# DeltaNet's V convolved token-major, with accumulating DMAs for the three lagged taps

## The reference

```python
def _causal_depthwise_conv(x, w):          # w is (4, channels)
    return lax.conv_general_dilated(
        x, w[:, None, :].astype(x.dtype), window_strides=(1,), padding=[(CONV_WIDTH - 1, 0)],
        dimension_numbers=('NWC', 'WIO', 'NWC'), feature_group_count=x.shape[-1])

proj = h @ w_in
qkv, z, b_pre, a_pre = _split(proj, L1_SPLITS)
qkv = jax.nn.silu(_causal_depthwise_conv(qkv, conv_w))
q, k, v = _split(qkv, [GDN_QK_W, GDN_QK_W, GDN_V_W])     # 2048, 2048 and 4096 channels
...
rhs = jnp.concatenate([v * beta[..., None], k_beta * jnp.exp(g_cum)[..., None]], axis=-1)
```

## Time and profile before

| | |
|---|---|
| three executions | 2725.23, 2725.53, 2725.72 us |
| span of the profiled execution | 2723.3 us |
| the profiled execution's own time | not given apart from the span; the median of the runs is 2.2 us above it |
| TensorE busy | 2707.9 us, 99% of the span |
| VectorE, ScalarE busy | 1807.0 us (66%), 1412.0 us (52%) |
| GpSimd busy | 94.2 us (3%) |
| DMA | 510.93 MB, mean 188 GB/s |
| granted clock of TensorE | full in all 40 slices |
| the four DeltaNet rounds | about 1226 to 1760 us of the span |

### The profile page before, as it was taken

The page is one execution under the profiler, slowest core; times in us unless marked ns, Lnnn a source line. Parts: engine busy times, 40 slices in busy tenths (PEclk is TensorE's granted clock), DMA queues, the critical chain, the costliest instruction groups (busy, mean ns, idle before and its releaser), DMA issues.

```text
span 2723.3 us, 37074 instructions
## 1 busy us (share of the span) xinstructions
PE 2707.9 (99%) x13198; PEld 2252.4 (83%) x13198; DVE 1807.0 (66%) x2538; ACT 1412.0 (52%) x2005; POOL 94.2 (3%) x80
## 2 busy tenths in 40 slices
PE   9999999999999999999999999999999999999998
PEld 7888888888888888888888888888888888888887
DVE  5554678666666666668797978656767666666444
ACT  5444555444444444458787778554454444444443
POOL 0000000000000000001111111000000000000000
PEclk9999999999999999999999999999999999999999
DMA  8564466766666666666464656555666666666664
GB/s 260 155 195 146 154 198 188 200 193 193 192 193 192 193 190 196 194 188 195 151 191 155 186 178 188 170 182 189 193 193 194 192 193 193 193 193 194 209 194 158
DMA packets 264737, 510.93 MB, mean 188 GB/s; under 512 B 20497, under 2 KB 21265, under 8 KB 264353
## 3 DMA queue, kind: packets, MB, share of 16 engines
q1 hardware_dynamic: 260064, 493.91, 60.0%
q0 software_dynamic: 3152, 11.57, 1.3%
q10 hardware_dynamic: 1392, 3.77, 0.4%
HBM read 503.91 MB, written 5.28 MB: 187 GB/s over the span
## 4 chain that ended last, share of the span: by engine, by line
PE 96%; DVE 2%; ACT 0%; issue 0%; DVEq 0%; DMA 0%; SPq 0%; ACTq 0%
PE acc L602 30%; PE acc L603 30%; PE acc L608 30%; PE aux L843 1%; DVE wlo L1541 1%; PE aux L687 1%; PE aux L855 1%; PE aux L848 1%; PE aux L837 0%; PE aux L829 0%; DVE const L1986 0%; DVE arena L1986 0%; DVE arena L2027 0%; DVE arena L2024 0%; DMA x<-in_x 0%
## 5 line engine op out<-in xcount | busy, mean ns | idle before, releaser
L1541 DVE TENSOR_TENSOR wlo<-wraw,whi 128x1024 fp32r<-128x1024 f32 x928 | 1137.0, 1233 | 711.0 <-ACT whi L1052 704.8
L1052 ACT ACTIVATE whi<-wraw 128x1024 fp32r<-128x1024 f32 x928 | 978.5, 1059 | 1101.8 <-PE acc L608 1059.5
L602 PE MATMUL acc<-whi,hT_hi 128*128 128x512 f32 x2624 | 1033.9, 394 | 0.5 <-ACT arena L1062 0.5
L603 PE MATMUL acc<-whi,hT_lo 128*128 128x512 f32 x2624 | 1022.8, 390 | 0.0
L608 PE MATMUL acc<-wlo,hT_hi 128*128 128x512 f32 x2624 | 702.8, 390 | 0.5 <-DVE wlo L1541 0.5
L608 PEld LDWEIGHTS acc<-wlo,hT_hi 128*128 128x128 f32 x2624 | 492.0, 188 | 103.7 <-DVE wlo L1541 1.3
L602 PEld LDWEIGHTS acc<-whi,hT_hi 128*128 128x128 f32 x2624 | 493.3, 188 | 101.9 <-ACT arena L1062 0.8
L603 PEld LDWEIGHTS acc<-whi,hT_lo 128*128 128x128 f32 x2624 | 493.4, 188 | 100.1
L602 PE MATMUL acc<-whi,arena 128*128 128x512 f32 x1072 | 417.2, 389 | 0.0
L603 PE MATMUL acc<-whi,arena 128*128 128x512 f32 x1072 | 417.0, 389 | 0.0
L608 PE MATMUL acc<-wlo,arena 128*128 128x512 f32 x1072 | 286.5, 389 | 0.0
(11 more groups left out here) (269 smaller groups left out, 1202.3 us busy)
## 6 DMA issues: line engine op xcount, KB each, us to landing
wraw<-in_l_w_in SPq DMA_DIRECT2D x304, 512.0 KB, 4.3
wraw<-in_l_w_gate SPq DMA_DIRECT2D x176, 512.0 KB, 4.3
wraw<-in_l_w_up SPq DMA_DIRECT2D x176, 512.0 KB, 4.3
wraw<-in_l_w_down SPq DMA_DIRECT2D x176, 512.0 KB, 4.3
wraw<-in_l_w_out SPq DMA_DIRECT2D x96, 512.0 KB, 4.5
arena<-decay_sums POOLq DMA_DIRECT2D x16, 512.0 KB, 5.1
o_rounds<-arena POOLq DMA_DIRECT2D x3, 1024.0 KB, 5.5
arena<-o_rounds ACTq DMA_DIRECT2D x3, 1024.0 KB, 5.2
```

Of the source, the lines that this page charges most:

```text
L602: nc.tensor.matmul(pair[m], hi[:, k, tok], wh, start=first, stop=False)
L603: nc.tensor.matmul(pair[m], lo[:, k, tok], wh, start=False, stop=False)
L1052: nc.scalar.activation(whi[:, s, :], wraw[:, s, :], ACT.Copy).then_inc(hi_done, 1)
L1541: V.tensor_tensor(wlo[:, s, :], wraw[:, s, :], whi[:, s, :].bitcast(F32), ALU.subtract).then_inc(lo_done, 1)
```

## The change

V0 and V1 are no longer turned. They are convolved where they lie, token-major. There a tap is a row of 512 weights, the same for all partitions, and a lag is an offset of one to three partitions, which crosses from token half 0 to half 1. VectorE multiplies the block by the four rows of weights, in two parts of two multiplications, at slots 1 and 2 for V0 and 20 and 21 for V1. The product with the last tap goes to `v_conv_sum`, the others to `weighted[0..2]`. For each lag GpSimd issues two DMAs that add SBUF to SBUF: the rows 0 to 127 - lag go `lag` partitions down, and the last `lag` rows of the first half go to the first rows of the second half. It waits for the two of one lag before it issues those of the next. Then ScalarE applies silu to the sum at the slot where `silu(V0)` was (7), and at 28 for V1, and scales the rows into `v_tok` from there.

The buffers come out of `x`: its 16 KB per partition are stored to DRAM when layer 1 begins and loaded back behind the last round. A DMA brings the four rows of weights of each V block, broadcast to all partitions (1 MB written).

```diff
-TOK_AT = counts(K, V0, Q, V1)
-CONV_TR_AT = lambda r, b: b + 1 if r == 0 else 3 * r + 1 + b
+TOK_AT = counts(K, Q)
+CONV_TR_AT = lambda r, b: 1 if b == K else r + 2
+V_BLOCK = lambda r, b: 2 * r + (b == V1)
+V_SUM_AT = lambda r, b: 32 * (CW - 1) * (V_BLOCK(r, b) + 1)
...
+        xflat = x[:, :, :].rearrange("p m n -> p (m n)")
+        k_spare = at(44 * KB, [P, M, NB])
+        weighted = [xflat[:, 2 * NB * l:2 * NB * (l + 1)].rearrange("p (m n) -> p m n", m=M) for l in range(2)]
+        weighted.append(k_spare[:, :, :])
+        v_conv_sum = C["decay"].rearrange("p (m n) -> p m n", m=M)
+        tap_rows = xflat[:, 4 * NB:8 * NB].rearrange("p (w n) -> p w n", w=CW)
...
 GpSimd
+            def store_x():
+                pool.wait_ge(xs_copied, 8)
+                pool.dma_start(x_dram[:, :], xflat).then_inc(x_stored, 16)
+            def load_x():
+                pool.wait_ge(v_sum, V_SUM_AT(ROUNDS - 1, V1))
+                pool.dma_start(xflat, x_dram[:, :]).then_inc(x_back, 16)
+            def taps(r, b):
+                n, col = V_BLOCK(r, b), P * conv_tile(r, b)
+                if n:
+                    pool.wait_ge(v_weighted, n)
+                else:
+                    pool.wait_ge(x_stored, 16)
+                pool.dma_start(tap_rows, A["conv_rows"][:, col:col + NB].rearrange("(a w) n -> a w n", a=1).to_broadcast([P, CW, NB])
+                               ).then_inc(taps_in, 16)
+            def lags(r, b):
+                n = V_BLOCK(r, b)
+                pool.wait_ge(v_weighted, n + 1)
+                for lag in range(1, CW):
+                    src, done = weighted[lag - 1], 32 * ((CW - 1) * n + lag)
+                    pool.dma_start(v_conv_sum[lag:, :, :], src[0:P - lag, :, :], accum_op=ALU.add).then_inc(v_sum, 16)
+                    pool.dma_start(v_conv_sum[0:lag, 1, :], src[P - lag:, 0, :], accum_op=ALU.add).then_inc(v_sum, 16)
+                    if lag < CW - 1:
+                        pool.wait_ge(v_sum, done)
             def gdn(r):
                 pool.wait_ge(a_set, D_AT(r, 1))
                 nc.gpsimd.memset(TT[:], 0.0).then_inc(tt_zero, 1)
                 nc.gpsimd.memset(T[:], 0.0)
+                taps(r, V1)
...
                 a.then_inc(t_in, 1)
+                lags(r, V1)
                 pool.wait_ge(lev_psum, LEVEL_PSUM(r, "q64_0"))
...
                     pool.wait_ge(lev_psum, LEVEL_PSUM(r, "TT64_1"))
+                    taps(r + 1, V0)
                     decay_rows(r + 1)
                     decay_columns(r + 1)
+                    lags(r + 1, V0)
                     pool.wait_ge(o_normed, r + 1)
...
             keep_x("dn0")
+            store_x()
+            taps(0, V0)
...
             decay_columns(0)
+            lags(0, V0)
             for r in range(ROUNDS):
                 gdn(r)
+            load_x()
 TensorE
-                if s == 0:
-                    if r:
-                        pe.wait_ge(end_dve, END_DVE(r - 1, "o1"))
-                    conv_transposes(V0, aux[1])
                 if s == 4:
                     if r:
                         pe.wait_ge(end_act, END_ACT(r - 1, "vn1"))
+                        pe.wait_ge(end_dve, END_DVE(r - 1, "o1"))
                     pe.wait_ge(conv_sum, TOK_AT(r, K))
                     token_major(K, aux[0])
-                    pe.wait_ge(conv_sum, TOK_AT(r, V0))
                     products(4, aux[1])
-                if s == 10:
+                if s == 15:
                     pe.wait_ge(tok_copy, TOK_AT(r, K))
-                    token_major(V0, aux[0])
-                if s == 15:
-                    pe.wait_ge(tok_copy, TOK_AT(r, V0))
                     conv_transposes(Q, aux[0])
-                if s == 27:
-                    pe.wait_ge(kq_mask, r + 1)
-                    conv_transposes(V1, aux[0])
-                if s == 31:
-                    pe.wait_ge(conv_sum, TOK_AT(r, V1))
-                    token_major(V1, aux[0])
                 if s == 32:
+                    pe.wait_ge(kq_mask, r + 1)
-                    pe.wait_ge(tok_copy, TOK_AT(r, V1))
+                    pe.wait_ge(v_rows, V_BLOCK(r, V1) + 1)
 ScalarE
+                def v_rows_silu(b):
+                    act.wait_ge(v_sum, V_SUM_AT(r, b))
+                    nc.scalar.activation(flat(v_conv_sum), flat(v_conv_sum), ACT.Silu).then_inc(v_silu, 1)
                 def value_rows(b):
-                    act.wait_ge(tok_tr, TOK_AT(r, b))
+                    act.wait_ge(v_silu, V_BLOCK(r, b) + 1)
+                    act.wait_ge(a_set, D_AT(r, 1))
...
                 if s == 2:
-                    tap(V0)
                     silu(K)
...
                 if s == 7:
-                    silu(V0)
+                    v_rows_silu(V0)
                 if s == 28:
-                    tap(V1)
+                    v_rows_silu(V1)
-                if s == 31:
-                    silu(V1)
-                if s == 32:
+                if s == 30:
                     act.wait_ge(et_set, r + 1)
                     value_rows(V1)
 VectorE
+                def v_conv(b, part):
+                    n, v = V_BLOCK(r, b), qkv[:, :, v_cols(b)]
+                    if part == 0:
+                        dve.wait_ge(taps_in, 16 * (n + 1))
+                        dve.wait_ge(acc_read[b % 2], (BLOCK0["l1"] + 4 * r + b) // 2 + 1)
+                        if n:
+                            dve.wait_ge(v_rows, n)
+                            dve.wait_ge(v_sum, 32 * (CW - 1) * n)
+                    for lag in (2 * part, 2 * part + 1):
+                        tap = tap_rows[:, CW - 1 - lag, :].unsqueeze(1).to_broadcast([P, M, NB])
+                        a = V.tensor_tensor(weighted[lag - 1] if lag else v_conv_sum, v, tap, ALU.mult)
+                    if part == 1:
+                        a.then_inc(v_weighted, 1)
-                if s == 2:
-                    conv(V0)
+                if s in (1, 2):
+                    v_conv(V0, s - 1)
...
                 if s == 22:
                     conv(Q)
+                if s in (20, 21):
+                    v_conv(V1, s - 20)
-                if s == 27:
-                    conv(V1)
```

More of the change, by code:

```diff
@@ L256, in build @@
         qkT = at(28 * KB, [P, 8, SEQ])
-        vT = C["decay"].rearrange("p (t n) -> p t n", n=SEQ)
+        weighted = [xflat[:, 2 * NB * l:2 * NB * (l + 1)].rearrange("p (m n) -> p m n", m=M) for l in range(2)]
+        weighted.append(k_spare[:, :, :])
+        v_conv_sum = C["decay"].rearrange("p (m n) -> p m n", m=M)
+        tap_rows = xflat[:, 4 * NB:8 * NB].rearrange("p (w n) -> p w n", w=CW)
         k_turned = at(36 * KB, [P, 4, SEQ])
@@ L284, in build @@
         sums_T = at(64 * KB, [P, P])
+        x_dram = nc.dram_tensor("x_saved", (P, M * D), F32, kind="Internal").ap()
         o_dram = nc.dram_tensor("o_rounds", (SEQ, VH * GD), F32, kind="Internal").ap()
@@ L298, in build @@
         aux = [ctx.enter_context(nc.psum_tensor(f"aux{i}", [P, 2 * NB], F32)) for i in range(2)]
-        conv_in = lambda r, b: flat(k_turned) if b == K and r else (aux[0], aux[1], aux[0], aux[0])[b]
+        conv_in = lambda r, b: flat(k_turned) if b == K and r else aux[0]
         aux4 = [aux[i // 2][:, (i % 2) * NB:(i % 2 + 1) * NB] for i in range(4)]
@@ L346, in build @@
         conv_silu = sem("conv_silu")
+        x_stored = sem("x_stored")
+        x_back = sem("x_back")
+        taps_in = sem("taps_in")
+        v_weighted = sem("v_weighted")
+        v_sum = sem("v_sum")
+        v_silu = sem("v_silu")
+        v_rows = sem("v_rows")
         tok_tr = sem("tok_tr")
@@ L421, in build @@
         conv_tile = lambda r, b: (QKH + HQ * r, 2 * QKH + HV * r, HQ * r, 2 * QKH + HV * r + 4)[b]
-        conv_out = (qkT[:, 4:8], vT, qkT[:, 0:4], vT)
+        conv_out = {K: qkT[:, 4:8], Q: qkT[:, 0:4]}
+        v_cols = lambda b: slice(b * NB, (b + 1) * NB)
         block = ctx.enter_context(nc.Block())
@@ L1349, in value_rows @@
                             n = HV * c + 4 * (b == V1) + h
-                            a = nc.scalar.activation(v_tok[int(b == V1)][:, c, h, :], aux[0][:, c * NB + h * P:c * NB + (h + 1) * P], ACT.Copy,
-                                                     scale=small(3, n, 1))
-                    a.then_inc(tok_copy, 1)
+                            a = nc.scalar.activation(v_tok[int(b == V1)][:, c, h, :], v_conv_sum[:, c, head(h)], ACT.Copy, scale=small(3, n, 1))
+                    a.then_inc(v_rows, 1)
                 def level_copy(step, dst, rows, cols):
@@ L1367, in gdn @@
                 if s == 2:
-                    tap(V0)
                     silu(K)
-                    if r == ROUNDS - 1:
-                        act.wait_ge(conv_tr, CONV_TR_AT(r, V0))
-                        load_o(0)
                 if s == 5:
@@ L1380, in gdn @@
                 if s == 7:
-                    silu(V0)
+                    v_rows_silu(V0)
+                    if r == ROUNDS - 1:
+                        load_o(0)
                 if s == 9:
```

(5 more changed lines are left out.)

## The result

The changed kernel takes 2842.35 us (median of five, 2839.59 to 2848.53) against 2725.53: ratio 1.0435, interval 1.0423 to 1.0447 (the ratios here and below are estimated from all executions, so they can differ by up to 0.2% from the quotient of two medians). It is slower by 116.8 us, where +50.4 was forecast. The direction and the range held; the size was off by more than a factor of two.

A forecast was written before the change was run, and what follows sets the result against it. TensorE, busy 99% of the span, was taken as the bound. V0's wait +47.1, VectorE's insertion +10.5 and the transposes saved -7.2 made +50.4 on 2725.5: 2776 us, range 2737 to 2985.

The forecast's parts named there:

- the bound and the place: TensorE, busy 99%, sets the pace; ScalarE idles ahead of V0's silu, with TensorE gaps after slot 9 and at 24 or 25.
- The turns: TensorE's transposes of V, 0.90 us per group of eight; V0's eight groups give nothing, V1's eight give 7.2 us.
- V0's wait: ScalarE's silu at slot 7 waits for three lags, late by 51.1 us; less 4 idle, 47.1 us reaches slot 25.
- three lags are 20.4 us: Three dependent lags behind VectorE's products, each taken at 6.8 us from GpSimd's pairs of DMAs from DRAM.
- S: Time of one lag on GpSimd: 6.8 us taken, ends 3.7 and 9.4; the sum is zero at 2.6.
- V1's wait: V1's silu behind its three lags ends at 1322.7; cost nothing at 6.8, about 8 us a round at 9.4.
- V1 costs nothing at 6.8: With 6.8 us a lag, V1's sum reaches TensorE's merge product in time; at 9.4 about 8 us a round.
- VectorE's insertion: V1's products at slots 20 and 21 delay `conv(Q)` by 4.88 us, 2.26 covered; 2.6 a round, 10.5 us.
- Taken at nothing: Output store behind V0's lags, weights' rows, decay DMAs, store and load of `x`: zero; 1 to 3 us each if uncovered.
- C: Rival: the adding is slow but spread, S at 9.4; +81.6 and V1's 8 us a round, 2839; inside the forecast's 0.64.
- A: Rival, slot 7: DMAs in time, S under 2.6; 2711, or 2721.6 if `conv(Q)` isn't covered; chance 0.08 faster, 0.03 unchanged.
- B: Rival: a lag uses few DMA engines, so 6.8 us becomes 30.7; +242, 2967, or 3171 at half rate; chance 0.25.

The follow-up runs named there:

- e3: The changed kernel without the lag DMAs, so V is convolved by its last tap alone; VectorE's four products stay: 2749.26 us, ratio 1.0086.
- e10: e3 with VectorE making only one of the four products of a V block: 2724.63 us, ratio 0.9995 to the kernel before.
- e2: The changed kernel with GpSimd issuing V0's lags ahead of its decay columns instead of behind them: 2855.29 us, ratio 1.0466.
- e4: The changed kernel with the lag DMAs as plain copies that overwrite instead of adding: 2804.61 us, ratio 1.0291.
- e1: The changed kernel with V0's silu and value rows moved from slots 7 and 13 to slot 15: 2831.44 us, ratio 1.0382.
- e8: The changed kernel with each large lag DMA moving 112 rows, down by 16 partitions, instead of 127, 126 and 125: 2838.11 us, ratio 1.0413.
- e6: e5 with V1's silu and value rows moved from slots 28 and 30 to slot 31: 2769.51 us, ratio 1.0162.
- e5: e1 with the store of a round's output ahead of the next round's V0 lags in GpSimd's list: 2799.5 us, ratio 1.0265.

## Why the prediction was right and wrong

**Right: the bound and the place.** TensorE had no slack, and what a silu behind a chain of three DMAs costs reached it. Leaving the lags out gives 93 us (e3). ScalarE stands ahead of V0's silu, TensorE has its gap at slot 9 (12.2 to 13.4 us, where some 6 were forecast), the busy share is 96% (97% forecast). The turns are worth about what was said: in V1's halves e10 gains 5.7 us, where 8 x 0.9 = 7.2 was the term.

**V0's wait, 47.1 forecast; V0's halves lost 68.1.** The step that failed is "three lags are 20.4 us" counted from the end of the products. From there to the last landing it was 26.8, 25.7, 25.6 and 25.7 us: 5.4 + 3 x 4.3 = 18.3 us in which the lags weren't issued, and 4 x 1.0 of longer lags. These 22.3 us are about the 21.0 that are missing. The prediction read how late VectorE's products were, and not how late the issuing engine was; the selects ahead of the lags were taken at their old price. Two things keep this from being a plain addition. With no lags V0's halves still lose 4.5 us (e3), which then must be hidden under the wait. And lags that start on time take longer (24.3 to 25.8 in e2): that three of them took 21.4, near the forecast, went with the stopped weight stream, which the prediction didn't foresee. The agreement in S was luck in part.

**V1's wait, nothing forecast, the largest miss.** The step "V1 costs nothing at 6.8" took one S for both blocks. S was 7.1 in V0 and 8.6 to 9.5 in V1. The step's own threshold held: with plain lags V1's S is 6.0 to 6.8 and V1's halves lose no more than with none (e4, 10.1 against 9.7). And the prediction's line for S = 9.4 (8 us a round, 32) has about the measured size: V1's halves lost 38.2, of which 28.5 go with the lags (38.2 - 9.7 in e3). What was mis-sized is S where the weight stream runs and the DMA adds.

**VectorE's insertion, 10.5 forecast, was too small.** e3 against e10: three of four products cost 4.5 + 4.2 = 8.7 us in V0's halves and 9.7 + 5.7 = 15.4 in V1's. With the 7.2 of the turns, V1's halves of e3 lost 9.7 + 7.2 = 16.9 where 10.5 was the term: the 2.26 us of cover ahead of silu(Q) weren't there, and 3.7 us more work a round cost 3.9. In V0 the new products only replace the old convolution in length (4.88 against 4.75), yet e3 lost 4.5 us there. That part was taken at nothing.

**Taken at nothing.** The start cost 9.5 us (0.9 of it was already there before 1165). The "1 to 3 us each" for an uncovered weights' row was too low at the one place without lead. The output store's zero held in the change and was 63 us of waiting in e1: it was hidden by another wait, not by slack.

**The sum, redone.** Start 9.5 (forecast 0), V0's halves 68.1 (47.1), V1's halves 38.2 (10.5 - 7.2 = 3.3): 115.8 against 50.4. C's 2839 is near the time, but partly by errors that cancel: its V0 is 12 x 9.4 - 34.5 = 78.3, 10 too high, it has no start (9.5), and its V1's halves, 32 + 3.3, are 3 too low.

**Rivals.** A is out: it wanted a lag under 2.6 us, and the shortest took 6.0; and with no lags at all and one product the kernel is only level with the one before (e10), since the start alone eats 9.4 of the 14.4 us. B is out (the steps, and e8). C is half right: adding is 38 us of the loss (e4), 28 of them in V1's halves.

**Left open:** whether the weight stream alone makes the lags slower where it runs, what of e6's loss in V0's halves isn't ScalarE's wait at slot 15, and whether `x` could be kept elsewhere.

## What to carry to other kernels

When a step moves to a DMA chain, price it from where the issuing engine's list lets the chain begin, and look at every instruction ahead of it on that engine for what the new work beside it does to its duration. Then ask what other transfers run at that moment: a chain that starts 4.3 us earlier can land only 1 us sooner (e2). A wait taken at nothing because another wait covers it returns in full as soon as that one is mended (e1), so repair such chains together (e5, e6). And where TensorE runs without a gap, a stall costs its length and, behind those of 3.6 to 13.4 us here, 3 to 7 us at half clock, so a saving of 0.9 us a piece on TensorE isn't worth one new wait.

## What the runs showed of the hardware that wasn't expected

- GpSimd's select of 128x1024 took 1.09 us undisturbed and up to 9.00 beside an unbroken row of VectorE instructions with two SBUF inputs, whose 128x1024 ones kept their 1.22 us: the select ended at the next break of that row. There a VectorE product of 128x16 took 1.08 us instead of 0.17.
- Beside GpSimd's three copies (1320.83 to 1324.98) VectorE's own product of 128x1024 took 1.62 us:

```profile
1324.44 1.62 DVE L2053 TENSOR_TENSOR x<-arena,x 128x1024 f32<-128x1024 f32 x1
```

- An accumulating DMA of 508 KB inside SBUF landed in 7.3 us, the plain one in 4.6; its issue took 0.86 to 0.94 us against 0.53 to 0.60.
- The accumulating DMA of 2 to 6 KB beside each landed in 6.0 to 8.2 us (medians), no sooner than the large one.
- Three dependent accumulating DMAs in a row took 21.3 to 21.5 us where the weights' queue ran dry during them, and 24.3 to 30.0 us in all other places of the changed kernel, e2 and e6.
- A row count of 127 didn't confine a DMA from GpSimd to one engine: its step took 8.3 to 9.9 us, and 112 rows instead changed the time by 4 us in 2842.
